# Reading gate and up weight columns with a step of eight, to give activations in the row order of the down weights

## What is computed

```python
logits = (h @ w_router + b_router)            # 32 experts, each token takes its top 4
gate = softmax(top 4 logits)
# for each expert e, on the tokens that chose it:
gu = xb @ w_gate_up[e] + b_gate_up[e]         # (1024) @ (1024, 2048)
g, lin = gu[:, :1024], gu[:, 1024:]
g = minimum(g, 7); lin = clip(lin, -7, 7)
act = g * sigmoid(1.702 * g) * (lin + 1.0)
y = act @ w_down[e] + b_down[e]               # (1024) @ (1024, 1024)
# output: sum over a token's experts of gate * y
```

## Time and profile before

| what | before |
|---|---|
| median of 2 runs | 1157.26 us (1153.28 to 1161.25) |
| the profiled execution | 1160.08 us |
| its span in the trace | 1158.3 us |
| TensorE busy (matmul) | 1125.1 us, 97% |
| TensorE weight loads | 496.3 us, 43% (overlap the matmuls) |
| VectorE busy | 289.1 us, 25% |
| ScalarE busy | 179.4 us, 15% |
| moved by DMA | 431.89 MB, mean 373 GB/s |

### The profile page before, as it was taken

One profiled execution on the slowest core, in us unless ns is written; L12 is line 12 of the kernel. 1 busy time (PEld: TensorE's weight loads), 2 busy tenths in 40 slices (PEclk: granted clock), 3 DMA queues, 4 the chain that ended last, 5 costly groups with the idle time before them and its releaser, 6 DMA issues.

```text
span 1158.3 us, 12748 instructions
## 1 busy us (share of the span) xinstructions
PE 1125.1 (97%) x4959; PEld 496.3 (43%) x4960; DVE 289.1 (25%) x661; ACT 179.4 (15%) x333; POOL 82.4 (7%) x155
## 2 busy tenths in 40 slices
PE   7998799899999999999999999999999999999997
PEld 6876586533333333333333333333333333333332
DVE  3999971311111111111111111111111111111112
ACT  3111030201111111111111111111111111111112
POOL 2975300000000000000000000000000000000000
PEclk9999899869999999999999999999999999999999
DMA  8734089549999999999999999999999999999994
GB/s 234 252 119 173 0 306 418 215 173 406 427 427 430 428 428 429 428 428 429 428 428 429 428 428 429 428 428 429 428 428 429 428 429 429 428 429 429 427 428 197
DMA packets 51618, 431.89 MB, mean 373 GB/s; under 512 B 6465, under 2 KB 22255, under 8 KB 25390
## 3 DMA queue, kind: packets, MB, share of 16 engines
q1 hardware_dynamic: 51598, 431.62, 89.8%
HBM read 430.56 MB, written 1.05 MB: 373 GB/s over the span
## 4 chain that ended last, share of the span: by engine, by line
PE 89%; DVE 9%; ACT 1%; issue 1%; DMA 0%; another core or an unknown queue 0%; DVEq 0%; SPq 0%; POOL 0%
PE bank L1280 38%; PE bank L1292 20%; PE bank L1300 10%; DVE bank L812 5%; PE bank L1253 5%; PE bank L1259 3%; PE bank L1078 3%; PE bank L1215 2%; PE bank L1180 2%; PE bank L1272 1%; DVE ring L844 1%; DVE ring L845 1%; PE bank L1246 1%; DVE ring L835 1%; PE bank L1264 1%; PE bank L1167 1%
## 5 line engine op out<-in xcount | busy, mean ns | idle before, releaser
L1280 PE MATMUL bank<-ring,area 128*64 128x512 f32 x2048 | 452.4, 594 | 1.0 <-DMA ring<-w_gate_up 1.0
L1280 PEld LDWEIGHTS bank<-ring,area 128*64 128x64 f32 x2048 | 147.6, 137 | 282.5 <-issue 273.3
L1292 PE MATMUL bank<-ring,area 128*64 128x512 f32 x1024 | 226.8, 595 | 1.0
L969 DVE TENSOR_SCALAR area<-bank 128x512 f32<-128x512 f32 x32 | 22.1, 691 | 772.8 <-PE bank L1280 772.8
L1292 PEld LDWEIGHTS bank<-ring,area 128*64 128x64 f32 x1024 | 70.7, 137 | 136.6 <-issue 127.9
L1300 PE MATMUL bank<-area,spT 128*128 128x512 f32 x256 | 118.4, 605 | 0.0
L1078 PE MATMUL bank<-area,ring 128*128 128x256 f32 x480 | 113.6, 399 | 1.2 <-DVE area L749 1.2
L1078 PEld LDWEIGHTS bank<-area,ring 128*128 128x128 f32 x480 | 95.4, 201 | 18.6 <-issue 2.3
L658 ACT ACTIVATE area<-area 128x512 f32<-128x512 f32 x32 | 20.1, 630 | 499.3 <-DVE area L969 499.3
L1300 PEld LDWEIGHTS bank<-area,spT 128*128 128x128 f32 x256 | 46.0, 189 | 71.9 <-issue 71.9
L812 DVE SCALAR_TENSOR_TENSOR bank<-ring,spread,bank 128x256 f32<-128x256 f32 x174 | 69.0, 480 | 0.0
(11 more groups left out here) (241 smaller groups left out, 552.1 us busy)
## 6 DMA issues: line engine op xcount, KB each, us to landing
ring<-w_gate_up SPq DMA_DIRECT2D x120, 2048.0 KB, 30.9
ring<-w_down SPq DMA_DIRECT2D x60, 2048.0 KB, 29.3
ring<-w_gate_up SPq DMA_DIRECT2D x16, 1024.0 KB, 12.2
ring<-w_in SPq DMA_DIRECT2D x15, 1024.0 KB, 9.6
ring<-w_down SPq DMA_DIRECT2D x8, 1024.0 KB, 13.3
ring<-w_out SPq DMA_DIRECT2D x1, 4096.0 KB, 14.1
ring<-w_conv_out SPq DMA_DIRECT2D x1, 3072.0 KB, 12.9
rows<-x SPq DMA_DIRECT2D x2, 512.0 KB, 3.6
```

The costliest lines, as they stand in the source:

```text
L969: return v.tensor_scalar(gc, bank[4][:, :], 7.0, None, ALU.min)
L1280: last = mm(bank[4 + b][64 * h:64 * h + 64, :], heT[:, k % 4, k // 4 * 64:k // 4 * 64 + 64], w[:, b * FF + h * 512:b * FF + h * 512 + 512] ...
L1292: last = mm(bank[6][64 * h:64 * h + 64, :], actT[:, k % 4, k // 4 * 64:k // 4 * 64 + 64], w[:, k % 2, h * 512:h * 512 + 512], start=(k == ...
```

## The change

The row order of `w_down` in SBUF becomes that of `w_gate_up`: partition `p` holds rows `8*p` to `8*p+7`, slot `c` of the four `w_down` slots holding rows `8*p + 2*c` and `8*p + 2*c + 1`. Sizes and number of the transfers stay; a pair still brings four neighbouring rows of 4 KB to each partition.

The activation therefore has to be at column block `k` for feature `8*p + k`. The change gets that by the order in which `gate_up` streams its columns: product `h` reads, of the 1024 columns of gate (or up), those with `k` from `4*h` to `4*h+3`, first all 128 with the first `k`, each 8 float32 from the one before, then the next `k`. The bias product reads its bfloat16 row in the same way. Then VectorE's `times_sigmoid` needs no permutation and becomes a plain product.

```diff
-        dn_v = w_down[0].rearrange("e (h p m) n -> e h p m n", p=128, m=4)
+        dn_v = w_down[0].rearrange("e (p k) n -> e p k n", p=128)
...
-                    src, dst = dn_v[e, c // 2, :, c % 2 * 2:c % 2 * 2 + 2, :], grid(at(half * PER + j, CH), 2, D)
+                    src, dst = dn_v[e, :, 2 * c:2 * c + 2, :], grid(at(half * PER + j, CH), 2, D)
...
-                    src, dst = dn_v[e, (j - KD) // 2], grid(at(half * PER + j, 2 * CH), 4, D)
+                    c = j - KD
+                    src, dst = dn_v[e, :, 2 * c:2 * c + 4, :], grid(at(half * PER + j, 2 * CH), 4, D)
...
             def times_sigmoid():
-                return v.tensor_tensor(gc.rearrange("a (m p) -> a p m", p=128), grid(lc, 128, 4), grid(sg, 128, 4), ALU.mult)
+                return v.tensor_tensor(gc, lc, sg, ALU.mult)
...
                 ks = range(KD) if part is None else range(4 * part, 4 * part + 4)
+                def columns(row, b, h):
+
+                    return row[:, b * FF:b * FF + FF].rearrange("a (p k) -> a k p", k=KD)[:, 4 * h:4 * h + 4, :]
+
                 for b in range(2 if 0 in ks else 0):
                     for h in range(2):
-                        mm(bank[4 + b][64 * h:64 * h + 64, :], onehot[:, buf, :], biasb[:, (2 * b + h) * 512:(2 * b + h + 1) * 512],
-                           start=True, stop=False)
+                        mm(bank[4 + b][64 * h:64 * h + 64, :], onehot[:, buf, :], columns(biasb, b, h), start=True, stop=False)
...
                             last = mm(bank[4 + b][64 * h:64 * h + 64, :], heT[:, k % 4, k // 4 * 64:k // 4 * 64 + 64],
-                                      w[:, b * FF + h * 512:b * FF + h * 512 + 512], start=False, stop=(k == KD - 1))
+                                      columns(w, b, h), start=False, stop=(k == KD - 1))
```

## The result

| what | before | after |
|---|---|---|
| median of 2 runs each | 1157.26 us | 1688.76 us (1688.6 to 1688.93) |
| ratio, with its 95% interval | | 1.46 (1.4535 to 1.4665) |
| span in the trace | 1158.3 us | 1686.9 us |

The kernel became slower by 46%. The direction was as forecast; 1609 us was not enough, and 1688.76 lies 24 us above the upper end of the range, 1665.

What follows compares the result with a forecast made beforehand. TensorE and DMA chains of about equal length were taken as the bound; 13.15 + 1.25 - 0.24 us an expert, +14.16, times 32 = 453 us, less 1.0 us of wait, gave 1612, on the median's scale 1609 us; range 1150 to 1665.

Steps and rivals of the forecast that it cites:

- What bounds the kernel: Expert loop: TensorE at 27.91 us and DMA at 29.4 us an expert, chains of about the same total length.
- VectorE's product: Product with the sigmoid: 684 ns instead of 1052, giving TensorE at most 0.24 us an expert.
- The loads of `w_down`: DMA loads with a source step of 32 KB instead of 16 between partitions: costed at nothing.
- The stepped reads: TensorE's gate_up and bias streams: 840 ns a pair instead of 429 and 215, adding 13.15 and 1.25 us an expert.
- Rival 1: Stepped float32 reads in gate and up cost TensorE nothing: 1157 us; chance 0.35, 0.33 after 0.02 went to faster.
- Rival 2: A mild penalty on gate and up, pairs between 459 and 767 ns: 1180 to 1515 us; chance 0.07.
- Rival 3: TensorE's two column halves share one fetch, a pair taking 2 x 840 ns: 2523 us; chance 0.07.
- Rival 4: TensorE's granted clock falls because the array idles between columns: 2049 us; chance 0.05.

Runs made afterwards that it cites:

- e1: Changed kernel with gate_up and its bias reading contiguous columns again, w_down order and plain sigmoid product kept: 1155.68 us, ratio to before 1.0001.
- e6: Kernel before with a plain sigmoid product and the four transposes of `gc` reading their stationary operand at a step of four float32: 1156.79 us, ratio 1.0001.
- e7: Kernel before with only the bias product of gate_up reading bfloat16 at a step of eight: 1197.7 us, ratio 1.0359.
- e4: Kernel before with stepped reads: gate_up's first half 2 float32, second half 4, down 16, bias 4 bfloat16: 1635.32 us.
- e5: Kernel before reading short runs every 8 columns: gate_up's first half 2 float32, second half 4, bias 2 bfloat16: 1184.29 us.
- e9: Kernel before with stepped reads: gate_up's first half 3 float32, second half 16, down 8, scatter 2, bias 16 bfloat16: 1792.47 us.
- e8: Kernel before with gate_up and its bias writing PSUM at a step of 128 float32, weight reads contiguous, plain sigmoid product: 1164.59 us, ratio 1.0055.
- e2: Kernel before with only the scatter, a single full-width stream, reading `yrow` at a step of eight float32: 1269.13 us.
- e3: Changed kernel with the left column half of gate_up reading contiguous columns, only the right half stepped, bias as in the changed kernel: 1697.76 us.

## Why the prediction was wrong in size and right in kind

**What bounds the kernel: right.** "A gain on TensorE is worth nearly nothing, a loss on TensorE is paid in full" was shown from both sides: e1 and e6 made TensorE's expert 0.15 to 0.18 us shorter at a ratio of 1.0001, e7 made it 1.36 us longer and 40 of 43 us came.

**VectorE's product: right, slightly large.** 692 ns against 684 forecast. TensorE got 0.17 to 0.18 us an expert instead of 0.24.

**The loads of `w_down` at nothing: right** (e1).

**The stepped reads: mechanism right, price too low. This is the step that failed.** TensorE's stream did fall to a price of the size that VectorE's rows show, and the price goes with the lines of SBUF that a read opens (e4, e5, e9); that both engines pay it for one reason is likely and not shown. But I took the read row, L935, 1.64 ns an element, 840 ns a pair; the pairs took 919 (1.79 ns), and each bias pair 890. The term was 13.15 + 1.25 us an expert and measured 15.65 + 1.35, together 2.6 us more, 83 us over the loop, which accounts for the whole miss of 80 us. L935 is a short reduction at a step of 128 bytes, with a fixed part that I could only borrow from other operations, so that it came within 9% is partly luck; at 64 bytes TensorE too is cheaper than at 32, and 128 was not run on it. The other row, L978's write at 1.73 ns, would have given 1662 us. I used that as the upper end, as if the dearest row of another engine were a bound for this one. It was no bound: 3% more a column put the result outside. A range around a price borrowed from another engine needs room above its dearest row.

**Rival 1 (the step is free) fell.** Its thought wasn't empty: float32's slower pace does hide something, namely a step of 2 and stepped PSUM writes (e4, e8). At one column a line it hides only the first 0.84 of 1.79 ns. **Rival 2** fell with the pace of the pairs. **Rival 3 (shared fetch)** fell in e2 and e3: a single stepped stream is no faster than two. **Rival 4 (clock)** fell: the granted clock was 1.00 from 300 to 1600 us.

## What to carry to other kernels

When the order of data has to be changed somewhere, put the step where few elements pass or where something slower hides it: here one VectorE product of 512 columns an expert, or four weight loads an expert (e6), and not 32 streamed pairs of products. Count the 16-byte lines that a streamed operand opens, at about 1.8 ns each, and compare with the array's pace for the type; with runs of four float32 kept together, a period of 32 bytes was free (e5). And before crediting a gain, ask whether the chain next to it, here the DMA's, ends at the same moment.

## What the runs showed of the hardware that I had not expected

- The price per opened line is nearly the same for float32 and bfloat16 (1.68 to 1.80 ns), so a stepped bfloat16 stream loses far more, relatively: 215 to 890 ns a pair, against 429 to 919.
- The two column halves pay side by side and not one after the other, and, by the likely reading of e3, one half can run several instructions ahead of its neighbour.
- A weight load of 128 stepped float32 columns became only 57 ns longer (203 against 146), where the line price would have made it about 225 ns, and the pace of the transposes changed by 0.03 us for four.
- A write into PSUM with a step of 512 bytes costs about 0.80 ns a column, visible for bfloat16 (410 ns a pair) and not for float32 (431).
